# A two-layer encoder trunk: the gated product opened by token blocks, idle products behind two norms, and the final mLSTM state inside the prompt's block

## The reference

```python
for layer in range(2):
    h = rms_norm(x, g[0])
    mix = s5_mixer(h, ...) if layer == 0 else mlstm_mixer(h, ...)
    x = x + rms_norm(mix, g[1])
    f = conv_ffn(rms_norm(x, g[2]), ...)
    x = x + rms_norm(f, g[3])

# the end of s5_mixer
ag = gelu(y) @ w_glu
out = ag[..., :D_MODEL] * sigmoid(ag[..., D_MODEL:])

# the state of mlstm_mixer, chunk by chunk; the last C and n are outputs
C_new = decay * C + einsum('blh,blhv,blhk->bhvk', wg, vc, kc)
n_new = decay * n + einsum('blh,blhk->bhk', wg, kc)
# and its end
out = (hs * silu(z)) @ w_down
```

## Time and profile before

| | |
|---|---|
| median of 3 runs | 3534.18 us (3528.38 to 3534.88) |
| profiled execution | 3529.76 us |
| its span, first to last instruction | 3528.0 us |
| TensorE, matmuls | busy 3297.6 us, 93% |
| VectorE | busy 1855.2 us, 53% |
| ScalarE | busy 1166.7 us, 33% |
| GpSimd | busy 511.5 us, 14% |
| DMA | 387.46 MB, 110 GB/s on average |

### The profile page before, as it was taken

One profiled execution on the slowest core, in us unless ns is written; L12 is line 12 of the kernel. 1 busy time (PEld: TensorE's weight loads), 2 busy tenths in 40 slices (PEclk: granted clock), 3 DMA queues, 4 the chain that ended last, 5 costly groups with the idle time before them and its releaser, 6 DMA issues. The chain is left out here.

```text
span 3528.0 us, 53363 instructions
## 1 busy us (share of the span) xinstructions
PE 3297.6 (93%) x20054; PEld 3161.1 (90%) x20054; DVE 1855.2 (53%) x2795; ACT 1166.7 (33%) x1905; POOL 511.5 (14%) x792
## 2 busy tenths in 40 slices
PE   5569989999999998999988999979999999999997
PEld 4469989999999998999986798979989999999997
DVE  7944655444444546322235666654655555555556
ACT  6333443323232233322245322224443222233222
POOL 2241011000000012000013333320010000000011
PEclk7789999999999999999999999999999999999999
DMA  3555521111111122333249522225534443434443
GB/s 86 143 133 151 154 90 42 43 43 42 37 42 43 43 76 87 117 107 108 103 153 318 185 78 79 84 81 141 168 120 135 133 128 122 132 118 131 132 137 126
DMA packets 396276, 387.46 MB, mean 110 GB/s; under 512 B 46100, under 2 KB 333144, under 8 KB 395928
## 3 DMA queue, kind: packets, MB, share of 16 engines
q1 hardware_dynamic: 370554, 321.96, 29.7%
q0 software_dynamic: 18336, 55.14, 4.8%
q10 hardware_dynamic: 7176, 7.35, 0.7%
HBM read 279.36 MB, written 102.63 MB: 108 GB/s over the span
## 5 line engine op out<-in xcount | busy, mean ns | idle before, releaser
L1286 PE MATMUL pair<-x_head,w_head 128*128 128x384 f32 x2496 | 845.4, 339 | 31.0 <-DVE x_rest L1162 13.6
L1286 PE MATMUL pair<-x_rest,w_head 128*128 128x384 f32 x2496 | 841.5, 337 | 6.1 <-issue 6.1
L1286 PE MATMUL pair<-x_head,w_rest 128*128 128x384 f32 x2496 | 841.2, 337 | 0.0
L1609 DVE SCALAR_TENSOR_TENSOR cv<-u,par,cv 128x1024 f32<-128x1024 f32 x176 | 225.6, 1282 | 664.2 <-ACT u L1550 664.2
L898 DVE TENSOR_TENSOR w_rest<-w_raw,w_head 128x1024 fp32r<-128x1024 f32 x256 | 312.9, 1223 | 442.2 <-ACT w_head L894 441.9
L1286 PEld LDWEIGHTS pair<-x_head,w_head 128*128 128x128 f32 x2496 | 473.7, 190 | 39.3 <-issue 16.0
L1286 PEld LDWEIGHTS pair<-x_rest,w_head 128*128 128x128 f32 x2496 | 474.5, 190 | 8.6 <-issue 7.0
L1286 PEld LDWEIGHTS pair<-x_head,w_rest 128*128 128x128 f32 x2496 | 473.6, 190 | 0.0
L894 ACT ACTIVATE w_head<-w_raw 128x1024 fp32r<-128x1024 f32 x256 | 271.6, 1062 | 556.9 <-PE pair L1511 276.7
L1545 ACT ACTIVATE cv<-pair,par 128x384 f32<-128x384 f32 x264 | 177.1, 671 | 614.6 <-PE pair L1286 600.0
L1511 PE MATMUL pair<-a_head,w_head 128*128 128x384 f32 x1056 | 359.4, 340 | 9.6 <-DVE f L1642 7.8
(11 more groups left out here) (501 smaller groups left out, 5055.6 us busy)
## 6 DMA issues: line engine op xcount, KB each, us to landing
w_raw<-in_ffn_w_up_dram SPq DMA_DIRECT2D x88, 512.0 KB, 3.9
hs<-in_state_mlstm_C_dram SPq DMA_DIRECT2D x32, 1024.0 KB, 8.5
c_room<-in_state_mlstm_C_dram SPq DMA_DIRECT2D x64, 512.0 KB, 5.3
out_dram<-c_room SPq DMA_DIRECT2D x64, 512.0 KB, 4.6
w_raw<-in_mlstm_w_down_dram SPq DMA_DIRECT2D x48, 512.0 KB, 4.1
w_raw<-in_s_w_glu_dram SPq DMA_DIRECT2D x44, 512.0 KB, 4.1
w_raw<-in_ffn_w_down_dram SPq DMA_DIRECT2D x44, 512.0 KB, 3.7
w_raw<-in_mlstm_w_up_dram SPq DMA_DIRECT2D x32, 512.0 KB, 4.4
```

The lines of the kernel that those rows point to most:

```text
L1286: m = pe.matmul(out[:, 0:TB], lhs[slot][:, P * k:P * k + P], rhs[:, k, TB * c:TB * c + TB], start=(k == 0 and q == 0), stop=(k == KD - 1 a ...
L1609: ins = dve.scalar_tensor_tensor(out=cp, in0=up[:, j:j + SEQ], scalar=tw, in1=cp, op0=ALU.mult, op1=ALU.add)
```

## The change

Three parts, the first two in `front`, the last one from the prompt to `back`.

The opening of the gated product no longer waits for the last y banks at its start. For input tiles 0 to 4 it makes blocks 0 and 1; then it waits for those banks (`last_banks_free`) and makes block 2 for the same tiles; tiles 5 and 6 as before; for tile 7 the three gates come before the three values, and the semaphore counts follow.

`Norm.idle` issues products of the identity with ones into bank 6 which nobody reads: 10 behind the gated product, 15 behind the last spread of each of the two norms in `front`.

The final state moves into the prompt's block. The first three of its sixteen blocks come before TensorE's last transposes of the prompt, the others behind them, with the banks in another order. SP issues the first two weight loads of the down-projection when the first block of products is made, and loads 3 and 4 behind the last stores. ScalarE and VectorE make weight tiles 0 and 1 and the first four pairs of heads and remainders between their evictions. `Weights` and `Down` are made before the block, at addresses of their own, and their semaphores outlive the phase. `back` starts with the parameters' stack and goes on with weights from the third step.

```diff
-    def new_phase(self):
+    def new_phase(self, keep=()):
         self.nc.all_engine_barrier()
-        self.nc.clear_and_free_semaphores(self.held)
+        self.nc.clear_and_free_semaphores([s for s in self.held if s not in keep])
         self.nc.all_engine_barrier()
-        self.held = []
+        self.held = list(keep)
...
         pe.wait_ge(kept, 2 * NBAT)
         pe.wait_ge(ended, 4)
+
+    def last_banks_free(pe):
+
         pe.wait_ge(gelued, 4 * NBAT - 2)
...
+    def idle(self, pe, count):
+
+        for _ in range(count):
+            pe.matmul(self.env.bank[6][:, 0:P], self.env.ident[:, :], self.env.ones[:, :], start=True, stop=True)
...
-    def tensor_first(self, pe, h_ready):
+    def tensor_first(self, pe, h_ready, last_banks_free):
+
         for h in range(2):
-            w.ready(pe, h)
-        for k in range(KD):
+            self.w.ready(pe, h)
+        for k in range(self.ALONE):
+            h_ready(pe, k)
+            for i in range(self.FIRST - 1):
+                for h in range(2):
+                    self.first_products(pe, i, k, h)
+        last_banks_free(pe)
+        for k in range(self.ALONE):
+            for h in range(2):
+                self.first_products(pe, self.FIRST - 1, k, h)
+        for k in range(self.ALONE, KD - 1):
             h_ready(pe, k)
             for i in range(self.FIRST):
                 for h in range(2):
...
+                    self.first_products(pe, i, k, h)
+        h_ready(pe, KD - 1)
+        for h in range(2):
+            for i in range(self.FIRST):
+                self.first_products(pe, i, KD - 1, h).then_inc(self.opened if i < self.FIRST - 1 else self.w.used, 1)
...
-            eng.wait_ge(self.opened, 2 * i + h + 1)
+            eng.wait_ge(self.opened, (self.FIRST - 1) * h + i + 1)
...
                     norm1.spread(pe, g + m // 4)
+            norm1.idle(pe, 10)
             pe.wait_ge(glu.gated, steps)
             pe.wait_ge(glu.free, steps)
...
             norm1.spread(pe, 5)
+            norm1.idle(pe, 15)
             up_first(0, 2)
             up_first(1, 2)
...
             norm2.spread(pe, 5)
+            norm2.idle(pe, 15)
             next_first(0, 2)
             next_first(1, 2)
...
+        def shut_bank(n):
+
+            return bank[(1, 2, 3, 0, 4, 5, 6, 7)[n % 8]]
...
                 steps(sp, body)
+                sp.wait_ge(t_c, 1)
+                down.sync(sp, 0)
+                store(sp, 0)
+                for h in range(HEADS):
+                    sp.wait_ge(kept_c[0], BLOCKS // 2 + h + 1)
+                    sp.dma_start(n_out[0, 0, h:h + 1, :], nrow[h]).then_inc(s_n, 16)
+                down.sync(sp, 1)
+                for k in range(R):
+                    sp.wait_ge(s_c[k], 16 * (BLOCKS // R))
+                sp.wait_ge(s_n, 16 * HEADS)
...
+                    if not nxt:
+                        for n in range(BEFORE):
+                            shut_products(pe, n)
                     ge(pe, normed, c, h, 1, 1)
...
                 steps(pe, body)
+                pe.wait_ge(joined, STEPS_ALL)
+                pe.wait_ge(updated, HT * STEPS_ALL)
+                for n in range(BEFORE, BLOCKS):
+                    shut_products(pe, n)
+                for h in range(HEADS):
+                    shut_rows(pe, h)
...
                 steps(act, body)
+                for n in range(0, BLOCKS, 2):
+                    keep(act, n)
+                    if n == 6:
+                        down.w.round(act, 0, 0, first=True)
+                        act.wait_ge(finished, STEPS_ALL)
+                    if n == 8:
+                        down.w.round(act, 1, 1, first=True)
+                    if n >= 6 and n < 14:
+                        down.heads(act, (n - 6) // 2)
+                for h in range(HEADS):
+                    act.wait_ge(t_c, BLOCKS + h + 1)
+                    act.activation(nrow[h], shut_bank(4 + h)[0:1, :], ACT.Copy).then_inc(kept_c[0], 1)
...
                 steps(pool, body)
+                store(pool, 1)
...
                 steps(dve, body)
+                for n in range(1, BLOCKS, 2):
+                    keep(dve, n)
+                    if n == 7:
+                        down.w.subtract(dve, 0, 0, first=True)
+                    if n >= 7 and n < 15:
+                        down.rests(dve, (n - 7) // 2)
+                dve.wait_ge(t_c, BLOCKS + HEADS)
+                down.w.subtract(dve, 1, 1, first=True)
...
         def _(sp):
-            for k in range(steps):
+            params.sync(sp)
+            for k in range(2, steps):
                 down.sync(sp, k)
-                if k == 1:
-                    params.sync(sp)
...
         def _(act):
-            for q in range(4):
-                down.heads(act, q)
-            w.round(act, 0, 0, first=True)
             for q in range(4, down.PAIRS):
                 down.heads(act, q)
-            w.round(act, 1, 1, first=True)
...
         def _(dve):
-            for q in range(4):
-                down.rests(dve, q)
-            w.subtract(dve, 0, 0, first=True)
             for q in range(4, down.PAIRS):
                 down.rests(dve, q)
-            w.subtract(dve, 1, 1, first=True)
```

More of the change, by code:

```diff
@@ L864, with __init__ @@
 class Weights:
[L870 removed]
+    def __init__(self, env, places=None):
         self.at = env.nc.sbuf_base
[L872 to L874 removed]
+        if places is None:
+            places = [self.at + 4 * D * k for k in range(6)]
+            env.sb("w_room", [P, 6 * D])
+        self.raw = [env.at(f"w_raw{k}", [P, D], places[k]) for k in range(2)]
+        self.head = [env.at(f"w_head{k}", [P, D], places[2 + k], F32R) for k in range(2)]
+        self.rest = [env.at(f"w_rest{k}", [P, D], places[4 + k], F32R) for k in range(2)]
         self.landed = [env.sem(f"w_landed{k}") for k in range(2)]
@@ L1319, in sync, with first_products @@
             self.w.load(sp, self.unit(i, h), h, self.src[:, :, col:col + P], first=(i == 0))
-    def tensor_first(self, pe, h_ready):
+    def first_products(self, pe, i, k, h):
         w = self.w
-        for h in range(2):
-            w.ready(pe, h)
-        for k in range(KD):
+        for lhs, rhs, q in ((w.head, self.x_head, 0), (w.head, self.x_rest, 1), (w.rest, self.x_head, 2)):
+            m = pe.matmul(self.pair(i)[h][:, 0:TB], lhs[h][:, P * k:P * k + P], rhs[:, k, TB * i:TB * i + TB],
+                          start=(k == 0 and q == 0), stop=(k == KD - 1 and q == 2))
+        return m
+    def tensor_first(self, pe, h_ready, last_banks_free):
+        for h in range(2):
+            self.w.ready(pe, h)
[9 more added lines that the diff above has]
+        for k in range(self.ALONE, KD - 1):
             h_ready(pe, k)
```

145 lines of the change are left out of this document (59 added, 86 removed).

## The result

The changed kernel takes 3506.4 us (median of 7 runs, 3502.0 to 3517.2), the kernel before 3528.4 us beside it (7 runs, 3524.7 to 3534.9). The ratio is 0.9938 with a 95% interval of 0.9925 to 0.9952: 22 us less, 17 to 26 by the interval. Five more runs of the changed kernel gave 0.9944 (0.9932 to 0.9957).

A forecast was written before the change was run, and what follows sets the result against it. The prediction took TensorE, busy 93% of the span, as the bound. Its terms 3.5 + 1.25 + 2.4 + 13.4 + 1.7 = 22.25 us, taken from a median of 3534.2, gave 3512.0 us, range 3503 to 3521.

The forecast's parts named there:

- Opening, 3.5 us: Gated product's opening: block order removes the wait for late banks, so the third gate starts 3.5 us earlier (bounds 2.8 to 5.2).
- So TensorE goes on at 238.6 without a gap: Gated product's opening: blocks 0 and 1 need only free banks, so the 2.8 us gap after the y products goes.
- So nothing gives the time back: Behind all four changed places TensorE sets the pace with little idle time, so the 22.25 us stay won.
- Idle products, 1.25 + 2.4 us: At two norms: idle products hidden in TensorE's waits keep the clock up, saving 1.25 us and 2.4 us (bounds 0 to 6.5).
- The rival that the clock is not bought: At the norms: remaining small gaps still bring low clock, so 3.65 us are missing, 3515.6 us; chance 0.12.
- Final state, 13.4 us: Final state in the prompt's block with early weights: down-projection starts at 2360.7 instead of 2374.05, 13.4 us (bounds 6.9 to 15).
- B: End of the prompt's block: evictions, weight copies and stores make it a new wait, half of 13.4 left, 3518.7 us; chance 0.12.
- Third down step, 1.7 us: Down-projection's third step: weights no longer land late behind the parameters' stack, saving the 1.7 us stall (bounds 0 to 1.7).
- C: Third down step: the parameters' stack still delays the weights, the 1.7 us stall stays, 3513.7 us; chance 0.06.
- D: Prompt's block: state stores and two weight tiles share DMA engines at a cut rate, so the kernel is slower, 3540 us; chance 0.03.
- E: Opening gains only its idle time, idle products add time where waits are shorter; with B, 3524 us; chance 0.03.
- F: At the gaps with idle products: the clock falls at more of them in the median's executions, more gain, 3507 us; chance 0.06.

The follow-up runs named there:

- e11: The kernel before, unchanged, profiled once more: 3531.65 us (one run).
- e2: The kernel before with only the final state moved into the prompt's block and early down-projection weights; opening and norms as before: 3523.02 us, ratio 0.9977.
- e4: The kernel before with only the idle products (10, 15, 15) added: 3521.62 us, ratio 0.9974.
- e5: The kernel before with 25 unread products put into the very first part, where TensorE waits anyway: 3517.84 us, ratio 0.9972.
- e6: The kernel before with 40 unread products put into the very first part, where TensorE waits anyway: 3524.41 us, ratio 0.9996.
- e3: The kernel before with only the gated product's new opening: 3528.6 us, ratio 0.9999.
- e7: The changed kernel with the first two down steps' weights and first four pairs made behind the block boundary again: 3518.46 us, ratio 0.9967 to the kernel before.
- e1: The changed kernel run and profiled once more, as it is: 3507.97 us, ratio 0.9944 to the kernel before.
- e8: The changed kernel with the last token block's four residual loads issued one per down step from the 18th: 3507.11 us, ratio 0.9931 to the kernel before.
- e10: The changed kernel with paced residual loads and 15 idle products behind the third norm's last spread: 3509.97 us, ratio 0.9936 to the kernel before.
- e12: The changed kernel with paced residual loads and 5 wide idle products behind the third norm's last spread: 3498.37 us, ratio 0.9915 to the kernel before.

## Why the prediction was right, and where only its total was

The time, 3506.4 us, lies in the range of 3503 to 3521, and against the kernel before beside it the change took off 22 us, as in my sum. (The forecast of 3512.0 stood on a median of 3534.2 from three runs; seven gave 3528.4.) But that total is made of other terms than mine: a term of some 9 to 13 us that I did not have stands against an opening that brought nothing and a state's part that measured smaller. That they nearly cancel is luck.

- **Opening, 3.5 us: wrong.** The gap is gone in every profile with the new order, and the gain does not show. Two steps failed.
  - "So TensorE goes on at 238.6 without a gap" is true, but what it saves was taken from one execution. In the six profiles of the old order (before, e11, e2, e4, e5, e6) the gap is 2.81, 2.04, 0, 0, 2.84 and 2.35 us. ScalarE's gelus of the last banks stand behind its copy of tile 5, which waits for a transfer. In four of the six the gated product starts 3.1 us after that copy does; in e2 and e4 the y products end later than that, and there is no gap. From the y products' end to the product behind the gates it is 30.0 us on average in these six (27.5 to 31.9) and 27.9 in the eight of the new order (27.6 to 29.0): 2.1 us gained there, not 3.5.
  - "So nothing gives the time back" failed behind it. From the y products' end to the first product behind the fourth spread of the first norm (455.97 in the profile of before) it is 215.0 us on average in the six and 215.7 in the eight. The clock is no longer low at the opening (it was in before, e5 and e6), but it is low in the 4.2 us behind the gates in seven of the eight (0.59 to 0.65), against two of the six (e2, e4). And in six of the eight TensorE has a wait of 0.9 to 1.9 us some 10 to 12 us further on that no profile of the old order has. Why that wait comes stays open.

  e3's 0.4 us fits this, but its interval would hold the 3.5 us as well.
- **Idle products, 1.25 + 2.4 us: right in mechanism, not term by term.** First norm 1.4 us (12.4 to 11.0). Second norm 1.6 us (10.9 to 9.4) and 0.6 against e11: there the new order of waits, 0.94 and then 0.55 us for remainders, keeps a part of it. The first ten I had put at 0, since the clock stayed up behind that gap of 3.0 us in the one profile that I had. It is at 0.60 to 0.66 there in five of the seven profiles without the ten products, and 1.00 in all seven with them. The same 4.3 us in e11 and in e4:

```profile
464.00:468.30 4.30, 4.26 (x16) 4.29 (x17) 3.27 (x4) 3.19 (x5) 0.71 (x1) 0.62 0.42 144
```

```profile
463.70:468.00 4.30, 4.24 (x24) 4.27 (x25) 3.25 (x4) 3.22 (x5) 0.71 (x1) 1.00 0.45 152
```

From the fourth spread's product to the last block's first product it is 47.7 us in those five and 46.2 in the other nine, so the ten bring 1.6 us where the clock would fall. The rival that the clock is not bought is out: the clock is 1.00 in the window shown behind the first norm.

- **First FFN stage, not in the sum: the largest error.** "Behind all four places TensorE sets the pace (the idle time there is small), so nothing gives the time back" looked only at what could be lost behind the four places, not at what could be won there. The three waits of 2.0 us and the low clock behind them stood in the trace of before, 6 us of idle time under "issue". I took them as belonging to the loop. They belong to its place in the program: they are there in four profiles and absent in ten. In the traces 9 to 13 us went with them. In the times it was 9.9 us in e5 and 1.4 in e6, so what they are worth in an execution is known less well than that they go.
- **Final state, 13.4 us: right in the trace.** My steps against the rows shown: three blocks 2.7 us, measured 2.84; wait for the bank about 1, measured 0.78; thirteen blocks 11.9, measured 11.88; rows 3.65, measured 3.66; boundary 3.8, measured 4.63. From the transposes' end to the down-projection it is 20.9 us instead of 36.5; less the 2.84 us that were put ahead of the transposes, 12.8 us. The cover held: B, the block's end as a new wait, did not come in the traces. The early weights were sized well too, 5.6 us in e7 against my 6.5.
- **Third down step, 1.7 us: right, with a smaller size.** The wait is absent in e1, e2 and the first profile after. In the six profiles in which the state's part is the old one it was 1.73, 0.94, 0.66, 2.10, 0.46 and 0.88 us, 1.1 on average. C is out.
- **Together the state's part should be 15.1 us; alone it measured 8.1 [4.2, 12.0].** The trace's 14 us are outside this interval. Beside the idle products (the changed kernel against e4) it is 11 to 13 us. What takes back some 5 us in e2's executions stays open. The candidates are the stretches that vary by execution: the one up to the prompt's end by 11 us (without the products put ahead of the transposes), the down stage by 8.
- **Down stage.** It looked like a loss of 6.4 us in the profile after, and is none: it is the race of eight residual loads with the step's weights, which the first profile of before happened to win. One profile is one draw. With the paced loads of e8, e10 and e12 the longest wait of the stage is 1.33 us.

D and E did not come: nothing is slower, and the idle products end before the remainders. F, more from the clock, came in part: the 1.6 us at the first gap, in five profiles of seven. The larger extra time came from the loop.

## What to carry to other kernels

A gap in one profile is worth something only if what comes before it isn't itself waiting on something that varies: look where the chain rejoins, in more than one profile, before the gap is counted. When a change adds or removes instructions ahead of a hardware loop, compare the loop's back-edges before crediting the edit with the time: here 25 products that do nothing, in a place where TensorE idles, took three waits away and brought as much (9.9 us) as the whole set of idle products (9.2), though 40 in the same place took the same waits away and brought 1.4. Another 15, ahead of the next loop, brought three such waits into it, and its stage took 911.0 us where it takes 907.8 without them (e8) and 906.6 with 5 wide ones. So idle work that keeps the clock up is better made of few, wide products, of which one pair of kernels is the evidence (e10, e12). Bursts of bulk loads are better paced against the steps whose weights are loaded beside them: e8 shows that in the trace, and its time does not tell it from the changed kernel's. And count a gain only where the chain rejoins further on, too: the opening won 2.1 us and had none of it left before the first norm.

## What the runs showed of the hardware

Waits at a loop's back-edge, of 1.0 to 2.3 us, depended on where the loop's instructions lie. The profile lists transfers of instructions on a queue of their own. In the 10 us around the first back-edge of the kernel before (DMA view, 762 to 772 us) the second row gives GB/s in 40 slices:

```profile
DMA  0000000200000000000030000000000458999963
GB/s 0 0 0 0 0 0 0 66 0 0 0 0 0 0 0 0 0 0 0 0 66 0 0 0 0 0 0 0 0 0 20 137 156 233 250 266 328 340 207 113
...
q8 instruction: 2, 0.03, 1.6%
```

The second of the two instruction transfers (0.25 us at 66 GB/s, 16 KB) is in the slice from 767.0 us; TensorE stops at 767.7 and goes on at 769.72. In the second profile such a transfer is in the slice from 765.0; TensorE stops at 765.9 and goes on at 767.45. But e5, which has no wait there, has the same pair, in the slices from 762.0 and 765.5 of its view of 758 to 768 us, around its turn's first product at 765.2:

```profile
GB/s 166 82 23 23 20 23 12 0 0 0 0 0 0 0 0 0 66 0 0 0 0 0 0 0 0 0 0 0 0 0 66 0 0 0 0 0 0 0 0 29
```

So the transfer alone does not make the wait. What differs is when the next one comes: 5.0 us later in the kernel before and 10.3 in e5. That TensorE comes to the end of the instructions it has, four products into the turn, and waits for the next 16 KB, fits all of this and the dependence on place. It is argued, not shown: no run changed the fetching itself.

The granted clock fell to its lower level, 1.2 GHz, after a wait of 2.0 us at the back-edges (it is 0.60, 0.68 and 0.50 on average in the 4.3 us behind them in the first profile of before), and after 2.44 us behind the opening of the changed kernel (0.59). Each of these three waits at a back-edge had another of 0.8 to 1.0 us some 3 us ahead of it. Gaps of one length in one place went both ways: 3.0 us at 467.6 left the clock up in two profiles and brought it down in five, and 2.31 us behind the gates left it up in before and brought it to 0.68 in e2. The length of the gap alone does not say which. After the third norm of e12, with waits of 0.97 and 0.60 us around idle products, it stayed up.
